# The opening of a two-block network on one core: token norm between the modulation blocks, scaling on two engines, small loads behind a wait

## The chip, the cores and the metric

The kernel runs on one core of one Trainium2 chip. The metric is the device time of one execution in microseconds. The kernel before took 2512.3 us (median of 3 runs, 2510.04 to 2513.72).

## The reference

A first block (diffusion-transformer style) and two layers of a second block work on 256 tokens of width 1024. Only the opening of the first block matters here. A modulation vector is made from the condition, `silu(c) @ w_ada + b_ada`, for the latent tokens and for the context tokens; its first 1024 values are a shift and the next 1024 a scale. Then

```
h     = rmsnorm(x,   g_mix_pre) * (1 + scale)   + shift       # 256 latent tokens
h_ctx = rmsnorm(ctx, g_mix_pre) * (1 + scale_c) + shift_c     # 256 context tokens
p     = concat(h, h_ctx) @ w_in                               # keys, values, gates, queries
```

The neighbourhood attention that follows adds a small learned table of relative biases, `rpb` (8 heads, 15 x 31 values), to its scores. Behind it come a matrix memory branch, a mixture of 32 experts, and the second block.

## The kernel before

Every engine has its own program, written out by hand; the only ordering between engines is by semaphores. Whatever stands behind a wait on an engine waits too. Activations lie transposed, width on the partitions (8 chunks of 128) and tokens along the free axis: `hAll[:, c, 0:256]` is chunk c of the latent tokens, `hAll[:, c, 256:512]` of the context tokens.

Weights go through a ring of 6 places of 2 MB, all issued by SyncE in a fixed order (L578 to L584): ada0 to ada3 (the four blocks of w_ada that give shift and scale), na_k, na_v, then rel0, rel1 (a constant table), ml_k, ml_v, each of the last four when its place is free. Place n is free when the slab n - 6 has been used: rel0 waits for the modulation block 0, rel1 for 1, ml_k for 2, ml_v for 3. Ahead of them SyncE loads x and ctx (L576, L577). ScalarE issues some 35 small loads of vectors and constants (L642 to L654) and can compute only after them. GpSimd issues 16 loads of parts of `rpb` into the tile `relrhs` (L2293: 31 partitions by 6 elements of 4 bytes, 8 heads twice) and one of the gate biases `bg` (L2295), from the start of the kernel on. [...]

TensorE's order in the opening (L1030 to L1099) is this. It turns the vectors and the 8 chunks of tokens. Then come four modulation blocks: `ada(i)` is 16 matmul instructions of 512 columns on slab ada_i (L1046), ScalarE copies the sums (L664, `ada_copy`), `ada_turn(i)` is 8 narrow ones that turn the copy (L1054), and VectorE adds the bias (L1737, L1738, `modulation`). Behind all four stands the norm: 16 matmul instructions add the squares over the width (L1068), ScalarE copies (L676), 8 narrow ones turn the sums (L1072), VectorE adds epsilon (L1748), ScalarE takes the root (L678), VectorE the reciprocal (L1750), and 8 matmul instructions spread the result over the partitions (L1077). VectorE multiplies the tokens by it (L1753, L1754: 16 operations, `xn_done` per chunk), ScalarE applies scale and shift (L683 latent, L685 context: 16 operations, `h_done` per chunk). TensorE waits for all 8 chunks and then makes the projections: na_k in 4 tiles (L1084), na_v in 4 tiles (L1114), ml_k, ml_v, and so on. After tile na_v0 stands the first of seven groups of small matmuls that build the bias from `relrhs` and rel0 (L1099, `rel_group`); `rel_group(0)` waits for all 16 loads of `rpb`.

Of the kernel before, what the change touches and what calls it, by code (L numbers as in the profile page):

```python
# [10 lines left out]
ALU = mybir.AluOpType  # L11
ACT = mybir.ActivationFunctionType
# [3 lines left out]
D = 1024  # L16
DC = D // P
T = 256
# [6 lines left out]
EPS = 1e-6  # L25
# [112 lines left out]
def build(nc, A, out):  # L138

    with ExitStack() as ctx:  # L140
# [3 lines left out]
        def sem(name):  # L144
            return ctx.enter_context(nc.semaphore(name))


        bank = [ctx.enter_context(nc.psum_tensor(f"bank{i}", [P, 512], F32)) for i in range(8)]
# [10 lines left out]
        xT = sb("xT", [P, DC, T])  # L159
        vT = sb("vT", [P, NV1])  # L160
        v2T = sb("v2T", [P, 2 * NV2])
        mod = sb("mod", [P, 48])
        modc = sb("modc", [P, 16])
        gains = sb("gains", [P, 2, DC])
        stage = sb("stage", [P, 64])
        colA = sb("colA", [P, 8])
# [221 lines left out]
        n_sum = sem("n_sum")  # L388
        n_par = sem("n_par")
        n_parc = sem("n_parc")  # L390
        par_done = sem("par_done")
        par_copied = sem("par_copied")
        ada_rows = sem("ada_rows")
        ada_copied = sem("ada_copied")
# [56 lines left out]
        gains_done = sem("gains_done")  # L451
        sq_done = sem("sq_done")
        sum_done = sem("sum_done")
        ms_done = sem("ms_done")
        root_done = sem("root_done")
        rstd_done = sem("rstd_done")
        rstd_row = sem("rstd_row")
        xn_done = sem("xn_done")
        h_done = sem("h_done")
        lin_done = sem("lin_done")  # L460
# [170 lines left out]
        def _(act):  # L631
# [27 lines left out]
            def ada_copy(i):  # L659

                act.wait_ge(ada_rows, i + 1)
                if i:
                    act.wait_ge(lin_done, G1[f"ada{i - 1}"] + 1)
                act.activation(adaRow[i], bank[G1[f"ada{i}"] % 4][:, :], ACT.Copy).then_inc(ada_copied, 1)  # L664
# [5 lines left out]
                act.activation(sq[:, c, T:512], hAll[:, c, T:512], ACT.Square).then_inc(sq_done, 1)  # L670
            act.wait_ge(vecs_turned, 2)
            act.activation(v2T[:, :], bank[6][:, 0:2 * NV2], ACT.Copy).then_inc(v2_copied, 1)
            for i in range(4):
                ada_copy(i)
            act.wait_ge(par_done, 1)
            act.activation(rstd, bank[6][:, :], ACT.Copy).then_inc(par_copied, 1)  # L676
            act.wait_ge(ms_done, 1)
            act.activation(colA[:, 0:4], colA[:, 0:4], ACT.Sqrt).then_inc(root_done, 1)  # L678

            act.wait_ge(gains_done, 1)  # L680
            for c in range(DC):
                act.wait_ge(xn_done, c + 1)
                act.activation(hAll[:, c, 0:T], hAll[:, c, 0:T], ACT.Identity, bias=mod[:, c:c + 1],  # L683
                               scale=gains[:, 0, c:c + 1])
                act.activation(hAll[:, c, T:512], hAll[:, c, T:512], ACT.Identity, bias=modc[:, c:c + 1],  # L685
                               scale=gains[:, 1, c:c + 1]).then_inc(h_done, 1)

# [120 lines left out]
            for c in range(DC):  # L808
                act.wait_ge(n_xn, c + 1)
                act.activation(h2T[:, c, :], tmpx[:, c, :], ACT.Identity, bias=mod[:, 24 + c:25 + c],  # L810
                               scale=gpre[:, c:c + 1]).then_inc(h2_done, 1)
# [201 lines left out]
        def _(pe):  # L1013
# [18 lines left out]
            for c in range(DC):  # L1032
                if c >= 4:
                    pe.wait_ge(x_copied, 2 * (c - 4) + 2)
                for t in range(4):
                    last = pe.transpose(bank[c % 4][:, t * P:(t + 1) * P], xin[:, t, c * P:(c + 1) * P], K["ident"][:, :])
# [4 lines left out]
            def ada(i):  # L1041
                w = slab(f"ada{i}")
                b = open_bank(f"ada{i}")
                for c in range(DC):
                    r = 32 * (c % 4)
                    last = pe.matmul(b[r:r + 32, :], scol[:, c, :], w[:, c, :], start=(c < 4), stop=(c >= 4), skip_group_check=True)  # L1046
                last.then_inc(ada_rows, 1)

            def ada_turn(i):

                pe.wait_ge(ada_copied, i + 1)
                b = bank[G1[f"ada{i}"] % 4]
                for m in range(4):
                    last = pe.matmul(b[:, 2 * m:2 * m + 2], adaRow[i][:, m * P:(m + 1) * P], K["pick"][:, :], start=True, stop=True)  # L1054
                last.then_inc(lin_done, 1)

            pe.wait_ge(silu_done, 1)
            for i in range(4):
                ada(i)
                if i:  # L1060
                    ada_turn(i - 1)
            ada_turn(3)

            pe.wait_ge(sq_done, DC)
            pe.wait_ge(v2_copied, 1)
            for c in range(DC):
                r = 32 * (c % 4)
                last = pe.matmul(bank[6][r:r + 32, :], ones[:, 0:32], sq[:, c, :], start=(c < 4), stop=(c >= 4), skip_group_check=True)  # L1068
            last.then_inc(par_done, 1)
            pe.wait_ge(par_copied, 1)  # L1070
            for t in range(4):
                last = pe.matmul(bank[6][:, t:t + 1], rstd[:, t * P:(t + 1) * P], K["pick"][:, 0:1], start=True, stop=True)  # L1072
            last.then_inc(sum_done, 1)

            pe.wait_ge(rstd_done, 1)
            for t in range(4):
                last = pe.matmul(bank[5][:, t * P:(t + 1) * P], colA[:, t:t + 1].to_broadcast([P, P]), K["ident"][:, :],  # L1077
                                 start=True, stop=True)
            last.then_inc(rstd_row, 1)

            def feat(name, w, m, half, rhs, dst, kc=DC, base=0):

                for c in range(kc):
                    last = pe.matmul(dst, w[:, c, base + m * P:base + (m + 1) * P], rhs(c), start=(c == 0), stop=(c == kc - 1))  # L1084
                return last

            for c in range(DC):
                pe.wait_ge(h_done, c + 1)
            def rel_group(b):

                if b == 0:
# [244 lines left out]
            for g in range(4):  # L1336
                pe.wait_ge(lin_act, emptied(G1["out3"])[1])
                for k in range(4):
                    c = 4 * (g % 2) + k
# [366 lines left out]
        def _(dve):  # L1706
# [23 lines left out]
            def modulation(i):  # L1730

                g = G1[f"ada{i}"]
                ps = bank[g % 4][:, 0:8].rearrange("p (m a) -> p m a", a=2)
                vb = vT[:, ba + 4 * i:ba + 4 * i + 4]
                dve.wait_ge(lin_done, g + 1)
                if i < 4:
                    dve.tensor_tensor(modc[:, 4 * i:4 * i + 4], ps[:, :, 1], vb, ALU.add)  # L1737
                dve.tensor_tensor(mod[:, 4 * i:4 * i + 4], ps[:, :, 0], vb, ALU.add).then_inc(lin_dve, 1)  # L1738

            for i in range(4):  # L1740
                modulation(i)
            dve.wait_ge(*emptied(G1["ada3"]))
            dve.scalar_tensor_tensor(out=gains[:, 0, :], in0=mod[:, 8:16], scalar=1.0, in1=vcol("g_mix_pre"),
                                     op0=ALU.add, op1=ALU.mult)
            dve.scalar_tensor_tensor(out=gains[:, 1, :], in0=modc[:, 8:16], scalar=1.0, in1=vcol("g_mix_pre"),
                                     op0=ALU.add, op1=ALU.mult).then_inc(gains_done, 1)
            dve.wait_ge(sum_done, 1)
            dve.tensor_scalar(colA[:, 0:4], bank[6][:, 0:4], 1.0 / D, EPS, ALU.mult, ALU.add).then_inc(ms_done, 1)  # L1748
            dve.wait_ge(root_done, 1)
            dve.reciprocal(colA[:, 0:4], colA[:, 0:4]).then_inc(rstd_done, 1)  # L1750
            dve.wait_ge(rstd_row, 1)
            for c in range(DC):
                dve.tensor_tensor(hAll[:, c, 0:T], xT[:, c, :], bank[5][:, 0:T], ALU.mult)  # L1753
                dve.tensor_tensor(hAll[:, c, T:512], hAll[:, c, T:512], bank[5][:, T:512], ALU.mult).then_inc(xn_done, 1)  # L1754

            dve.memset(mlV[:, :, 128:129], 1.0).then_inc(ones_set, 1)

# [527 lines left out]
        @block.gpsimd  # L2285
        def _(pool):

            pool.wait_ge(ones_set, 1)
            src = A["rpb"][0].rearrange("h r d -> d h r")
            with nc.allow_non_contiguous_dma(reason="a small table turned"):  # L2290
                for a in range(2):
                    for h in range(NA_H):
                        pool.dma_start(relrhs[31 * a:31 * a + 31, 6 * h:6 * h + 6], src[:, h, 5 - a:11 - a])\  # L2293
                            .then_inc(relrhs_in, 16)
                pool.dma_start(bg[:, :], A["b_mlstm_gates"][0].rearrange("a b -> (a b)").partition_broadcast(P)).then_inc(bg_in, 16)  # L2295

            pool.wait_ge(na_os, NA_H)
            for w, n in enumerate(("b_gate", "b_lin", "b_down")):
                for k in range(2):
                    src = A[n][0][:, 512 * k:512 * k + 512][None, :, :].to_broadcast([2, E, 512])  # L2300
                    pool.dma_start(braw[64 * k:64 * k + 64, w, :], src).then_inc(moe_const, 16)
            pool.wait_ge(ml_o, 2 * ML_H)
            pool.wait_ge(lin_done, G1["b_na3"] + 1)
            pool.dma_start(posi.bitcast(I32), A["positions_2"][0].partition_broadcast(P)).then_inc(pos_in, 16)
            pool.dma_start(wr, A["w_router"][0].rearrange("(c p) n -> p c n", p=P)).then_inc(moe_const, 16)
            pool.dma_start(brow, A["b_router"][0].partition_broadcast(P)).then_inc(moe_const, 16)
            for L in range(2):
                pool.dma_start(gaRaw[:, L, :].rearrange("p (c n) -> p c n", c=DC),
                               A["w_in_2"][L][:, C2["ga"]:C2["ga"] + GR].rearrange("(c p) n -> p c n", p=P)).then_inc(moe_const, 16)
            pool.wait_ge(ml_hts, ML_H)  # L2310
            pool.dma_start(biaspick, A["biaspick"]).then_inc(moe_const, 16)

            pool.wait_ge(bias_hi, 1)
            for k in range(2):
                r = slice(64 * k + 32, 64 * k + 64)
                pool.tensor_tensor(bparts[r, :, :], braw[r, :, :], bparts[r, :, :].bitcast(F32), ALU.subtract).then_inc(bias_lo, 1)
# [17 lines left out]
```

## Time and profile before

| | us |
|---|---|
| median of 3 runs | 2512.3 |
| profiled execution, whole | 2512.79 |
| its span in the profile | 2511.0 |
| TensorE busy | 2284.8 (91%) |
| VectorE busy | 752.2 (30%) |
| ScalarE busy | 636.0 (25%) |
| GpSimd busy | 44.8 (2%) |
| first projection (na_k) starts at | 67.83 |
| first bias group (`rel_group(0)`) starts at | 104.53 |

The span begins with the first instruction of the profile; the whole execution is 1.8 us longer. A matmul of 32-bit operands appears as two instructions (x16 for 8 chunks). [...] The opening is the first 105 us, 4% of the span.

### The profile page before, as it was taken

Reading aid. Unit: us, or ns where it says so; the run is one execution under the profiler, and the core shown is the slowest. Engines: PE = TensorE matmul, PEld = TensorE weight load, DVE = VectorE, ACT = ScalarE, POOL = GpSimd, SP = SyncE. Lnnn points to the kernel's source line nnn. Section 1 sums busy time; section 2 is a strip of 40 time slices with the busy share of each in tenths; the row PEclk is TensorE's granted clock in tenths of the full one; section 3 lists DMA queues with packets and bytes.
Section 4 is the critical chain, followed back from the end, with each engine's and each line's share of the span. In section 5 each row is a group of like instructions: output and inputs, shape, how many; then the busy total and the mean of one; then the engine's idle time right before and its main releaser. Section 6 shows DMA issues by size and latency. Waiting matters only on the chain.

```text
span 2511.0 us, 31285 instructions
## 1 busy us (share of the span) xinstructions
PE 2284.8 (91%) x13158; PEld 1564.7 (62%) x13158; DVE 752.2 (30%) x1189; ACT 636.0 (25%) x900; POOL 44.8 (2%) x35
## 2 busy tenths in 40 slices
PE   4999998789889988988898889999999799998998
PEld 2458667533333333333333379998899699987997
DVE  1001225321111111111111156433444454442453
ACT  2101432211111111111111144422333435413432
POOL 2100000100000000000000000000000000000000
PEclk8898999799999999999999989999899899998999
DMA  9434354279999999999999966671245345541542
GB/s 285 86 118 168 137 211 126 83 308 427 428 428 427 428 428 427 427 427 429 424 428 427 400 138 167 149 255 67 101 168 185 107 163 164 193 148 68 184 160 93
DMA packets 133833, 626.99 MB, mean 250 GB/s; under 512 B 9344, under 2 KB 17040, under 8 KB 108864
## 3 DMA queue, kind: packets, MB, share of 16 engines
q1 hardware_dynamic: 128672, 622.51, 65.4%
q0 software_dynamic: 2912, 1.44, 1.0%
q8 instruction: 112, 1.84, 0.3%
q10 hardware_dynamic: 2112, 0.99, 0.2%
q14 instruction: 25, 0.20, 0.0%
HBM read 623.69 MB, written 1.05 MB: 249 GB/s over the span
## 4 chain that ended last, share of the span: by engine, by line
PE 72%; DMA 20%; DVE 3%; issue 3%; ACT 2%; ACTq 0%; SPq 0%; DVEq 0%
DMA ring<-in_w_lin 17%; PE bank L1365 15%; PE bank L1084 13%; PE bank L1463 11%; PE bank L1663 10%; PE bank L1678 4%; PE bank L1114 2%; DMA ring<-in_w_ada 1%; PE bank L1487 1%; DMA ring<-in_w_in 1%; PE bank L1472 1%; PE bank L1378 1%; PE bank L1353 1%; PE bank L1179 1%; PE bank L1046 1%
## 5 line engine op out<-in xcount | busy, mean ns | idle before, releaser
L1365 PE MATMUL bank<-ring,arenaA 128*64 128x512 f32 x3072 | 692.4, 601 | 38.9 <-DMA ring<-in_w_lin 29.4
L1365 PEld LDWEIGHTS bank<-ring,arenaA 128*64 128x64 f32 x3072 | 211.5, 138 | 460.7 <-issue 392.2
L1084 PE MATMUL bank<-arenaA,ring 128*128 128x256 f32 (+1 forms) x1408 | 345.1, 405 | 14.5 <-ACT arenaA L685 9.2
L2091 DVE TENSOR_TENSOR ring_rounded<-ring,ring_rounded 128x2048 fp32r<-128x2048 f32 (+1 forms) x140 | 293.4, 2134 | 114.7 <-ACT ring_rounded L864 114.7
L1084 PEld LDWEIGHTS bank<-arenaA,ring 128*128 128x128 f32 x1408 | 270.7, 195 | 88.9 <-issue 38.6
L864 ACT ACTIVATE ring_rounded<-ring 128x2048 fp32r<-128x2048 f32 (+1 forms) x140 | 243.2, 1783 | 299.5 <-DMA ring<-in_w_in 81.8
L1463 PE MATMUL bank<-arena_rounded,ring_rounded 128*128 128x256 f32 x2496 | 308.1, 283 | 1.7 <-DVE ring_rounded L2091 1.7
L1463 PEld LDWEIGHTS bank<-arena_rounded,ring_rounded 128*128 128x128 f32 x2496 | 300.1, 190 | 6.0 <-issue 3.1
L1663 PE MATMUL bank<-arena_rounded,ring_rounded 128*128 128x256 f32 x2112 | 260.4, 287 | 2.2 <-ACT arena_rounded L989 2.2
L1663 PEld LDWEIGHTS bank<-arena_rounded,ring_rounded 128*128 128x128 f32 x2112 | 258.5, 194 | 4.3 <-ACT arena_rounded L989 2.8
L2037 DVE TENSOR_SCALAR arenaA<-bank 128x512 f32<-128x512 f32 x32 | 22.1, 692 | 504.1 <-PE bank L1365 504.1
L1678 PE MATMUL bank<-arena_rounded,ring_rounded 128*128 128x256 f32 x912 | 109.9, 283 | 2.3 <-DVE arenaA L2270 2.3
L1678 PEld LDWEIGHTS bank<-arena_rounded,ring_rounded 128*128 128x128 f32 x912 | 109.5, 192 | 2.7 <-issue 2.7
L879 ACT ACTIVATE arenaA<-bank 128x512 f32<-128x512 f32 (+1 forms) x88 | 51.3, 586 | 226.6 <-PE bank L1463 120.8
L845 ACT ACTIVATE arenaA<-bank 128x512 f32<-128x512 f32 x32 | 19.1, 597 | 330.7 <-PE bank L1409 330.7
L849 ACT ACTIVATE arenaA<-bank 64x512 f32<-64x512 f32 x64 | 37.9, 592 | 213.6 <-PE bank L1365 213.2
L843 ACT ACTIVATE arenaA<-arenaA 128x512 f32<-128x512 f32 x32 | 20.2, 630 | 264.3 <-DVE arenaA L2037 264.3
L2049 DVE TENSOR_SCALAR arenaA<-bank 128x512 f32<-128x512 f32 x32 | 22.1, 692 | 203.7 <-PE bank L1365 203.7
L1378 PE MATMUL bank<-arenaA 128*128 128x256 f32 x256 | 63.5, 392 | 7.8 <-ACT arenaA L849 5.5
L1378 PEld LDWEIGHTS bank<-arenaA 128*128 128x128 f32 x256 | 45.7, 189 | 32.4 <-issue 18.7
L1297 PE MATMUL bank<-arenaA,ones 128*32 128x256 f32 x176 | 32.5, 501 | 31.9 <-ACT arenaA L775 24.9
L1359 PE MATMUL bank<-arena_rounded 128*128 128x512 f32 x96 | 45.2, 471 | 17.8 <-issue 17.1
(338 smaller groups left out, 1658.8 us busy)
## 6 DMA issues: line engine op xcount, KB each, us to landing
ring<-in_w_gate SPq DMA_DIRECT2D x64, 2048.0 KB, 22.9
ring<-in_w_lin SPq DMA_DIRECT2D x64, 2048.0 KB, 25.3
ring<-in_w_down SPq DMA_DIRECT2D x64, 2048.0 KB, 21.7
ring<-in_w_in SPq DMA_DIRECT2D x41, 2048.0 KB, 10.7
ring<-in_w_ada SPq DMA_DIRECT2D x12, 2048.0 KB, 15.5
ring<-in_w_ffn_gate SPq DMA_DIRECT2D x10, 2048.0 KB, 7.8
ring<-in_w_ffn_up SPq DMA_DIRECT2D x10, 2048.0 KB, 7.7
ring<-in_w_ffn_down SPq DMA_DIRECT2D x12, 1536.0 KB, 6.6
```

The costliest lines, as they stand in the source:

```text
L849: ins = act.activation(yN[(i % 2) * SLOTS:(i % 2 + 1) * SLOTS, k, :], bank[5][k * SLOTS:(k + 1) * SLOTS, :], ACT.Copy)
L864: act.activation(place2(name + "_hi", ringR)[:, a:b, :], place2(name)[:, a:b, :], ACT.Copy).then_inc(w_hi, 1)
L879: act.activation(dst, src(b) if src else b, func, scale=scale).then_inc(c_act, 1)
L1084: last = pe.matmul(dst, w[:, c, base + m * P:base + (m + 1) * P], rhs(c), start=(c == 0), stop=(c == kc - 1))
L1114: last = pe.matmul(b[:, :], hAll[:, c, m * P:(m + 1) * P], w[:, c, :], start=(c == 0), stop=(c == DC - 1))
L1359: pe.matmul(bank[b][:, :], bias, bparts[:, w, :], start=True, stop=False, skip_group_check=True)
L1365: last = pe.matmul(bank[b][k * SLOTS:(k + 1) * SLOTS, :], lhsT(c), slot(j)[:, c % 4, k * 512:(k + 1) * 512], start=False, stop=(c == DC - ...
L1378: last = pe.matmul(bank[6 + g % 2][:, k * T:(k + 1) * T], yN[:, c // 4, (c % 4) * P:(c % 4 + 1) * P], selWT, start=True, stop=True)
L1463: last = pe.matmul(b[:, j * T:(j + 1) * T], w[:, c, m * P:(m + 1) * P], h[:, c, :], start=(part == 0 and c == 0 and j == 0), stop=(part == ...
L1663: last = pe.matmul(b[:, j * T:(j + 1) * T], w[:, c, m * P:(m + 1) * P], h[:, c, :], start=(part == 0 and c == 0 and j == 0), stop=(part == ...
L1678: last = pe.matmul(bank[m // 2][:, (m % 2) * T:(m % 2 + 1) * T], w[:, k, m * P:(m + 1) * P], h[:, c0 + k, :], start=(part == 0 and c0 + k ...
L2091: dve.tensor_tensor(place2(name, ringR)[:, a:b, :], w[:, a:b, :], hi[:, a:b, :], ALU.subtract).then_inc(w_lo, 1)
```

## The change

TensorE's order becomes: ada(0); sums of squares; ada(1), turn 0; turn of the sums; ada(2), turn 1; spread of the reciprocal; ada(3), turn 2, turn 3. ScalarE, VectorE follow this order. The scaling of the latent half goes from ScalarE to VectorE (new semaphore `h_lat`); ScalarE keeps the context half. The first tile of na_k waits for each chunk just before its matmul, no longer for all eight. GpSimd waits for `ada_rows` to reach 4, which the last matmul of ada(3) brings about, before it issues its 16 + 1 small loads.

```diff
 # ScalarE
-            for i in range(4):
-                ada_copy(i)
-            act.wait_ge(par_done, 1)
+            ada_copy(0)
+            act.wait_ge(sum_done, 1)
             act.activation(rstd, bank[6][:, :], ACT.Copy).then_inc(par_copied, 1)
+            ada_copy(1)
             act.wait_ge(ms_done, 1)
             act.activation(colA[:, 0:4], colA[:, 0:4], ACT.Sqrt).then_inc(root_done, 1)
+            ada_copy(2)
+            ada_copy(3)
             act.wait_ge(gains_done, 1)
             for c in range(DC):
                 act.wait_ge(xn_done, c + 1)
-                act.activation(hAll[:, c, 0:T], hAll[:, c, 0:T], ACT.Identity, bias=mod[:, c:c + 1],
-                               scale=gains[:, 0, c:c + 1])
                 act.activation(hAll[:, c, T:512], ...).then_inc(h_done, 1)
 # TensorE
-            for i in range(4):
-                ada(i)
-                if i:
-                    ada_turn(i - 1)
-            ada_turn(3)
-
+            ada(0)
             pe.wait_ge(sq_done, DC)
             pe.wait_ge(v2_copied, 1)
...
-            last.then_inc(par_done, 1)
+            last.then_inc(sum_done, 1)
+            ada(1)
+            ada_turn(0)
             pe.wait_ge(par_copied, 1)
...
             last.then_inc(sum_done, 1)
+            ada(2)
+            ada_turn(1)
             pe.wait_ge(rstd_done, 1)
...
-            last.then_inc(rstd_row, 1)
+            last.then_inc(sum_done, 1)
+            ada(3)
+            ada_turn(2)
+            ada_turn(3)
             def feat(name, w, m, half, rhs, dst, kc=DC, base=0):
                 for c in range(kc):
+                    if name == "na_k" and m == 0:
+                        pe.wait_ge(h_done, c + 1)
+                        pe.wait_ge(h_lat, c + 1)
                     last = pe.matmul(...)
-            for c in range(DC):
-                pe.wait_ge(h_done, c + 1)
 # VectorE
-            for i in range(4):
-                modulation(i)
+            modulation(0)
+            dve.wait_ge(sum_done, 2)
+            dve.tensor_scalar(colA[:, 0:4], bank[6][:, 0:4], 1.0 / D, EPS, ALU.mult, ALU.add).then_inc(ms_done, 1)
+            modulation(1)
+            dve.wait_ge(root_done, 1)
+            dve.reciprocal(colA[:, 0:4], colA[:, 0:4]).then_inc(rstd_done, 1)
+            dve.wait_ge(sum_done, 3)
+            for c in range(DC):
+                dve.tensor_tensor(hAll[:, c, 0:T], xT[:, c, :], bank[5][:, 0:T], ALU.mult)
+                dve.tensor_tensor(hAll[:, c, T:512], hAll[:, c, T:512], bank[5][:, T:512], ALU.mult).then_inc(xn_done, 1)
+            modulation(2)
+            modulation(3)
             (gains as before)
+            dve.wait_ge(gains_done, 1)
+            dve.wait_ge(xn_done, DC)
             for c in range(DC):
+                dve.tensor_scalar(hAll[:, c, 0:T], hAll[:, c, 0:T], gains[:, 0, c:c + 1], mod[:, c:c + 1], ALU.mult, ALU.add)\
+                    .then_inc(h_lat, 1)
 # GpSimd
             pool.wait_ge(ones_set, 1)
+            pool.wait_ge(ada_rows, 4)
             (the 16 loads of rpb, the load of bg)
```

## Rows read from the trace of the kernel before

**Rows 1.** Page, chain that ended last: shares of the span by engine, by line.
```profile
PE 72%; DMA 20%; DVE 3%; issue 3%; ACT 2%; ACTq 0%; SPq 0%; DVEq 0%
DMA ring<-in_w_lin 17%; PE bank L1365 15%; PE bank L1084 13%; PE bank L1463 11%; PE bank L1663 10%; PE bank L1678 4%; PE bank L1114 2%; DMA ring<-in_w_ada 1%; PE bank L1487 1%; DMA ring<-in_w_in 1%; PE bank L1472 1%; PE bank L1378 1%; PE bank L1353 1%; PE bank L1179 1%; PE bank L1046 1%
```
**Rows 2.** Chain in order of time, 0 to 260 us: start, length, what.
```profile
15.14 30.33 DMA ring<-in_w_ada
...
51.61 3.42 PE bank L1068 x16
...
67.83 29.90 PE bank L1084 x64
97.73 6.87 PE bank L1114 x16
104.60 2.36 PE bank L1099 x20
```
**Rows 3.** Timeline of TensorE: start, length, line, tiles, [idle before <- releaser].
```profile
26.10 1.92 PE L1046 MATMUL bank<-ring,scol 128*32 128x512 f32 x16 [1.18 <-DVE arenaA L1726]
30.06 2.48 PE L1046 MATMUL bank<-ring,scol 128*32 128x512 f32 x16 [2.03 <-DMA ring<-in_w_ada]
32.46 1.87 PE L1054 MATMUL bank<-k_pick,arenaA 128*128 128x2 f32 x8
35.97 3.64 PE L1046 MATMUL bank<-ring,scol 128*32 128x512 f32 x16 [1.64 <-DMA ring<-in_w_ada]
...
48.76 1.05 PE L1054 MATMUL bank<-k_pick,arenaA 128*128 128x2 f32 x8
...
57.46 1.16 PE L1077 MATMUL bank<-k_ident,colA 128*128 128x128 f32 x8 [0.71 <-DVE colA L1750]
```
**Rows 4.** Timeline of ScalarE, copy of v2T and first and last of 16 scalings.
```profile
26.62 0.24 ACT L672 ACTIVATE v2T<-bank 128x108 f32<-128x108 f32 x1
...
59.50 0.60 ACT L683 ACTIVATE arenaA<-arenaA,mod,gains 128x256 f32<-128x256 f32 x1 [2.31 <-DVE arenaA L1754]
...
66.89 0.58 ACT L685 ACTIVATE arenaA<-arenaA,modc,gains 128x256 f32<-128x256 f32 x1
```
**Rows 5.** Timeline of VectorE, first and last of 16 multiplications by the norm.
```profile
58.66 0.42 DVE L1753 TENSOR_TENSOR arenaA<-xT,bank 128x256 f32<-128x256 f32 x1 [1.25 <-PE bank L1077]
...
63.63 0.41 DVE L1754 TENSOR_TENSOR arenaA<-arenaA,bank 128x256 f32<-128x256 f32 x1
```
**Rows 6.** Timeline of GpSimd, five of the eight pairs of rpb loads.
```profile
1.41 3.73 POOL L2293 DMA_DIRECT2D arenaA<-in_rpb  x2 [0.95 <-DVE arenaA L1716]
15.60 3.53 POOL L2293 DMA_DIRECT2D arenaA<-in_rpb  x2 [10.46 <-issue]
...
71.66 3.53 POOL L2293 DMA_DIRECT2D arenaA<-in_rpb  x2 [11.18 <-issue]
84.99 3.53 POOL L2293 DMA_DIRECT2D arenaA<-in_rpb  x2 [9.80 <-issue]
93.67 3.52 POOL L2293 DMA_DIRECT2D arenaA<-in_rpb  x2 [5.14 <-issue]
```
**Rows 7.** DMA issues, us to landing: last rpb load (95.42), slab ml_v.
```profile
arenaA<-in_rpb POOLq DMA_DIRECT2D x1, 0.7 KB, 6.6
...
ring<-in_w_in SPq DMA_DIRECT2D x1, 2048.0 KB, 32.3
```
**Rows 8.** Windows: length, busy (count) by engine, PEclk, DMA share, GB/s.
```profile
8.00:11.00 3.00, 0.00 (x0) 0.00 (x0) 0.00 (x0) 0.00 (x0) 0.00 (x0) 1.00 0.99 118
...
15.00:21.00 6.00, 1.41 (x7) 1.01 (x5) 0.59 (x4) 3.04 (x4) 3.53 (x2) 1.00 1.07 369
21.00:25.00 4.00, 3.55 (x17) 3.33 (x17) 4.00 (x13) 3.65 (x12) 0.00 (x0) 1.00 1.24 117
...
35.00:39.00 4.00, 3.03 (x16) 0.59 (x16) 0.00 (x0) 0.03 (x1) 0.00 (x0) 0.50 1.30 114
```
**Rows 9.** The same windows view, TensorE's clock.
```profile
31.50:48.50 17.00, 11.25 (x56) 4.75 (x48) 0.46 (x4) 1.20 (x2) 5.08 (x3) 0.50 1.11 308
...
67.80:72.50 4.70, 4.67 (x6) 2.06 (x7) 0.00 (x0) 0.00 (x0) 0.84 (x1) 0.53 0.92 301
```

More of the change, by code:

```diff
@@ L390, in build @@
         n_parc = sem("n_parc")
-        par_done = sem("par_done")
         par_copied = sem("par_copied")
@@ L456, in build @@
         rstd_done = sem("rstd_done")
-        rstd_row = sem("rstd_row")
+        h_lat = sem("h_lat")
         xn_done = sem("xn_done")
@@ L1746, in _ @@
                                      op0=ALU.add, op1=ALU.mult).then_inc(gains_done, 1)
[L1747 to L1751, printed above, removed]
+            dve.wait_ge(gains_done, 1)
+            dve.wait_ge(xn_done, DC)
             for c in range(DC):
-                dve.tensor_tensor(hAll[:, c, 0:T], xT[:, c, :], bank[5][:, 0:T], ALU.mult)
-                dve.tensor_tensor(hAll[:, c, T:512], hAll[:, c, T:512], bank[5][:, T:512], ALU.mult).then_inc(xn_done, 1)
+                dve.tensor_scalar(hAll[:, c, 0:T], hAll[:, c, 0:T], gains[:, 0, c:c + 1], mod[:, c:c + 1], ALU.mult, ALU.add)\
+                    .then_inc(h_lat, 1)
             dve.memset(mlV[:, :, 128:129], 1.0).then_inc(ones_set, 1)
```

## The prediction

> **What bounds the kernel now.** I read the page first. The chain that ended last is 72% TensorE, 17% the stream of expert weights [rows 1]. There the reader sees that nothing on the page is about the opening: the change can only shift the moment from which everything behind it runs. So the question is when TensorE gets past the opening, and next I read the chain in order of time. It has two parts. Up to 45.5 us it waits for the fourth slab of w_ada (15.14 + 30.33 = 45.47), then runs the norm, one short step after another, and the scaling, until the first projection starts at 67.83. From there to 104.60 TensorE does nothing but projections, and then the first bias group [rows 2]. No DMA stands on this chain between 67.83 and 258 us, and the expert weights cannot start before their places are used by TensorE; so a shift of the moment at which the first bias group starts (104.6) passes on to the end in full.
>
> The third view is the timeline of GpSimd, an engine that the page shows at 2%. It issues the rpb loads in pairs, and between pairs it waits 5 to 11 us, put down to "issue" [rows 6]. The last load is issued at 95.42 (93.67 + half of 3.52) and lands 6.6 us later [rows 7], at 102.0. The bias group waits for all 16 and starts at 104.6: the loads, though they start at 1.41, have only 2.6 us to spare. This is the fact on which the forecast rests.
>
> The fourth view is the windows with the GB/s. Weights flow at 369 GB/s in 15 to 21 us, and at 118, 117 and 114 in 8 to 11, 21 to 25 and 35 to 39 us [rows 8], each about 6 us after a pair of rpb loads was begun. The small loads slow the slabs.
>
> **The change part by part.** Times are of the profiled execution (span 2511.0, whole 2512.8 us, 0.5 above the median of 2512.3).
>
> *Slabs come sooner.* Without rpb loads ahead of ada(3) the three slow stretches go: 3 x (1 - 118/369) = 2.0, 4 x (1 - 117/369) = 2.7, 4 x (1 - 114/369) = 2.8 us [rows 8], 7.5 us together. The fourth slab then lands at 38.0, not 45.5. If the slow stretches had another cause it stays 45.5; I take 38.0, since each of the three follows a pair. The second and third slabs were waited for at 30.06 and 35.97 [rows 3]; with 4.7 us less each (two stretches) they are there at 25.4 and 31.3.
>
> *TensorE's new order.* ada(0) can't start sooner than 26.10: it was released by VectorE's copies, not by a slab [rows 3]. It ends at 28.0. The squares are done (v2T copied at 26.9 [rows 4]), so the 16 matmuls of the sums follow, 1.9 us by ada(0)'s row, same shape, upper clock (3.42 at the lower [rows 2]): 29.9. ada(1) 1.9 (31.8), turn 0 1.05 (32.9), turn of the sums 1.05 by the same narrow form (33.9), ada(2) 1.9 (35.8), turn 1 1.05 (36.9), some 0.4 for modulation(1) and the reciprocal on VectorE, spread 1.2 [rows 3] (38.6), ada(3) 1.9: 40.5. With the lower clock, which was there from 31.5 to 48.5 [rows 9], the forms take 3.5 and 1.87 us (35.97 and 32.46 in [rows 3]): turn 0 33.7, turn of the sums 35.6, ada(2) 39.1, turn 1 41.0, spread about 43.2, ada(3) 46.7. Before the clock fell TensorE had waited for a slab; here it has hardly a gap from 26.1 on, so I take the upper: `ada_rows` is 4 at 41, bounds 39 and 47. All waits of ScalarE (copy of the sums, root with its table load) and VectorE lie beside these matmuls; they would show as gaps of under 1 us each.
>
> *Behind ada(3).* Turn 2 to 41.6, the copy of block 3 (0.6 and 0.2 of gaps), turn 3 to 43.5. VectorE's 16 multiplications go at 0.33 us ((63.63 - 58.66)/15 [rows 5]), 38.7 to 44.1, then two modulations and the gains, 0.4. They hide behind the turns but for 0.6 us or so. Scaling: ScalarE had 16 operations at 0.49 ((66.89 - 59.50)/15 [rows 4]), 7.9 us up to 67.47 before TensorE moved. Now it has 8, VectorE's 8 are beside them. No row shows that VectorE operation; bounded by 0.3 us (its multiplication) and 0.6 (ScalarE's), one chunk takes less than the 0.86 us that TensorE needs for its two matmuls of a chunk (6.87/8 [rows 2]), so the chunkwise wait costs TensorE one chunk at the most, 0.6 us. na_k starts at 45.3 (52 with the lower clock), where it was 67.83. Taken alone that is a gain of 15 to 22 us. From there five tiles at 6.87 us: TensorE stands at the bias group at 79.7 to 89.
>
> *The rpb loads, behind `ada_rows` >= 4.* They start at 41, not at 1.41. While slabs flow, a pair comes every 13.9 us ((84.99 - 1.41)/6); the one interval after the slabs were over is 8.7 us (84.99 to 93.67) [rows 6]. The slabs ended at 84.0 (ml_v is issued when the turn of block 3 is over, 51.6 [rows 2], and takes 32.3 to landing [rows 7]). They will end about 73, since in place of six pairs some two fall among them (four times 2.7). So the pairs start at 41, 54.9, 68.8, then with one mixed interval of 10 at 79, and at 87.7, 96.4, 105.1, 113.8; the last load is issued at 115.6 and lands at 122.2. TensorE stands still from about 80 to 122, and everything it gained is idle time. Nothing else can go ahead of the bias group on TensorE: na_v1 to the end are queued behind it, and ScalarE and VectorE wait for their banks. The group starts 17.6 us later than at 104.6.
>
> *The clock.* After the 9 us pause before 67.83 TensorE ran at 0.53 until 72.5 [rows 9]; the first four tiles took 29.90 us instead of 4 x 6.87 = 27.5, 2.4 lost [rows 2]. In the chain of before this loss stood ahead of 104.6; now a pause of 40 us stands right at the group, and I add 2.4 behind it (bounds 0 and 5).
>
> *Sum.* +17.6 + 2.4 = +20 us: 2512.8 + 20 = 2532.8, by the median 2532.
>
> [...]
>
> **Rivals.**
> (a) *The loads keep up, and the change is faster.* With nothing before them in the queues they may go faster than any pair of the trace did. From the start at 41, seven intervals and 8.4 us to the last landing (1.8 + 6.6): the result is no change in time when the landing is at 102.2 (104.6 less the 2.4 of the clock), which needs (102.2 - 41 - 8.4)/7 = 7.5 us a pair. [...] For it: only one interval without slabs is in the trace. Against it: that one is 8.7, and its parts leave little room (3.5 to issue the pair, the wait of 5.14 until the second has landed).
> (b) *No difference that can be told.* A pair of 6.5 to 8.2 us, 2512.3 within 5.
> (c) *The front is as slow as before and the loads still later.* The clock stays at the lower level from 31.5 on, `ada_rows` is 4 at 47, three intervals are of the loaded kind: 47 + 3 x 13.9 + 4 x 8.7 + 8.4 = 131.9, +27.3 and up to 5 of clock: 2545.
> (d) *All intervals are short.* 39 + 7 x 8.7 + 8.4 = 108.3, +3.7 + 2.4: 2518.
>
> **Chances.** The forecast with its neighbours (c) and (d), slower by 6 to 32 us, 0.86; (a) 0.10; (b) 0.04. A difference under 0.2% (5 us) can't be told from none. The likeliest is 2532, and the range 2517 to 2545 goes from (d) to (c) and leaves out (a) and (b), 14 in 100, and little more. Faster 0.10, same 0.04, slower 0.86.
>
> **What would show it.** In the profile after: ada(1) and ada(2) without waits for slabs, the fourth slab in by 38, GB/s near 370 without the low stretches until about 47; na_k starting at 45 to 52; GpSimd's first pair at about 41 and its last at about 114; TensorE with one idle stretch of 30 to 45 us before L1099, and at the lower clock for some us behind it; from there to the end the same length as before. I am wrong if that idle stretch is short or absent, which would be seen at once in pairs less than 7.5 us apart, or if part of the stall is given back later, which no row speaks for.

## The result and the profile after

The changed kernel took 2525.0 us (median of 5 runs, 2523.0 to 2530.0); the kernel before, measured with it on the same chip, 2510.5. The ratio is 1.0054, with a 95% interval of 1.0043 to 1.0066: 11 to 17 us slower. The forecast was 2532, slower. The profiled execution took 2523.0 us, its span is 2521.2 (2511.0 before). Two executions far off all others of their kernels, one of `e2_wait_only` (4531 us) and one of `e4_rows_old_order` (10334 us), are left out below.

First the timeline of TensorE after the change, opening only: start, length, line, tiles, count, and in brackets the idle time ahead and its releaser.

```profile
24.27 1.92 PE L1045 MATMUL bank<-ring,scol 128*32 128x512 f32 x16 [0.87 <-DVE arenaA L1727]
...
27.70 1.93 PE L1045 MATMUL bank<-ring,scol 128*32 128x512 f32 x16
...
31.44 1.92 PE L1045 MATMUL bank<-ring,scol 128*32 128x512 f32 x16
...
35.84 1.92 PE L1045 MATMUL bank<-ring,scol 128*32 128x512 f32 x16
...
42.78 30.30 PE L1087 MATMUL bank<-arenaA,ring 128*128 128x512 f32 x64 [2.23 <-DVE arenaA L1761]
72.91 7.03 PE L1115 MATMUL bank<-ring,arenaA 128*128 128x512 f32 x16
119.30 4.50 PE L1100 MATMUL bank<-arenaA,ring 63*128 63x48 f32 x20 [39.36 <-DMA arenaA<-in_rpb]
123.73 8.50 PE L1115 MATMUL bank<-ring,arenaA 128*128 128x512 f32 x16
```

The four modulation blocks (L1045) no longer wait for slabs; compare [rows 3]. The first projection starts at 42.78, 25 us sooner than in [rows 2], and TensorE is ready for the bias group at 79.9. Then it stands still for 39.36 us, until the last load of `rpb` (the small table of relative biases) has landed, and starts the group at 119.30: 14.8 us later than before, 104.5.

The timeline of GpSimd, to be held against [rows 6]:

```profile
38.59 3.73 POOL L2302 DMA_DIRECT2D arenaA<-in_rpb  x2 [38.13 <-PE bank L1045]
54.64 3.53 POOL L2302 DMA_DIRECT2D arenaA<-in_rpb  x2 [12.33 <-issue]
67.73 3.53 POOL L2302 DMA_DIRECT2D arenaA<-in_rpb  x2 [9.57 <-issue]
76.42 3.52 POOL L2302 DMA_DIRECT2D arenaA<-in_rpb  x2 [5.16 <-issue]
...
111.00 3.52 POOL L2302 DMA_DIRECT2D arenaA<-in_rpb  x2 [5.04 <-issue]
```

The pairs begin at 38.59 instead of 1.41; two intervals are long (16.1 and 13.1 us), the other five are 8.6 to 8.7. This chain is on the path to the end now, as the chain of waits of the changed kernel shows (start, length, what):

```profile
38.59 3.73 POOL arenaA L2302 x2
42.31 12.33 issue
...
111.00 1.75 POOL arenaA L2302
112.75 6.50 DMA arenaA<-in_rpb
119.30 4.50 PE bank L1100 x20
```

The windows (columns as in [rows 8]) show the weight stream at 387 GB/s up to the wait's end, the low stretch of 68 that begins 6 us after the pair of 54.64, and the pause:

```profile
29.00:41.00 12.00, 10.39 (x88) 6.57 (x80) 5.76 (x22) 3.28 (x5) 2.41 (x2) 1.00 1.05 387
...
60.50:63.50 3.00, 3.00 (x9) 1.33 (x8) 0.00 (x0) 0.00 (x0) 0.00 (x0) 1.00 1.24 68
...
82.00:119.00 37.00, 0.00 (x0) 0.00 (x0) 0.00 (x0) 0.00 (x0) 14.68 (x9) 0.50 0.48 3
119.00:124.00 5.00, 4.70 (x21) 4.61 (x22) 0.16 (x1) 0.00 (x0) 0.00 (x0) 0.50 0.00 0
```

PEclk, TensorE's granted clock, is 1.00 at what the prediction calls the upper clock and 0.50 at the lower: the same 16 matmuls of a modulation block took 1.92 us at 1.00 (31.44 above) and 3.64 at 0.50 (35.97 in [rows 3]).

Does the delay reach the end? SyncE's issues of the expert slabs (MOVE lines: first one is expert 1's) and of the second block's gate slabs are good milestones, since each is released by TensorE. Before:

```profile
L590 SPq MOVE ring<-in_w_gate x62: 29/29/29, 518.2 to 1392.9; - x62
L619 SPq DMA_DIRECT2D ring<-in_w_ffn_gate x12: 367/368/582, 1679.1 to 2392.5; - x12
```

After:

```profile
L589 SPq MOVE ring<-in_w_gate x62: 29/29/29, 533.3 to 1408.2; - x62
L618 SPq DMA_DIRECT2D ring<-in_w_ffn_gate x12: 367/368/582, 1694.6 to 2402.9; - x12
```

The delay is 14.8 us at the first bias group, 18.2 at the second (132.16 against 113.95), 16.5 from the third on (141.58 against 125.07), 15.1 at expert 1, 15.3 at the last, 15.5 at the second block. So it is passed on nearly whole. Within the second block this one execution wins 5.1 us back (708.3 us from first to last gate slab, 713.4 before), so that its span is only 10.2 longer; the medians differ by 14.5. The code there is the same, and in the runs this part varies from kernel to kernel, 701 to 714 us.

### The profile page after: what moved, and what is told of

It reads as the page before. It is cut to its first block, busy times and chain, and to the rows that moved or that the text cites. A ratio compares the mean times of both kernels' runs of the same rounds, so it can differ in the third digit from the quotient of the medians.

```text
span 2521.2 us, 31291 instructions
## 1 busy us (share of the span) xinstructions
PE 2278.9 (90%) x13158; PEld 1563.7 (62%) x13158; DVE 754.7 (30%) x1197; ACT 631.6 (25%) x892; POOL 44.7 (2%) x35
## 4 chain that ended last, share of the span: by engine, by line
PE 68%; DMA 20%; issue 4%; DVE 3%; ACT 2%; POOL 1%; ACTq 1%; DVEq 0%; POOLq 0%
DMA ring<-in_w_lin 19%; PE bank L1366 14%; PE bank L1087 12%; PE bank L1464 11%; PE bank L1664 10%; PE bank L1679 4%; PE bank L1115 2%; PE bank L1488 1%; POOL arenaA L2302 1%; DMA ring<-in_w_in 1%; PE bank L1045 1%; PE bank L1473 1%; PE bank L1379 1%; PE bank L1180 1%; PE bank L1691 1%
## 5 line engine op out<-in xcount | busy, mean ns | idle before, releaser
L2045 DVE TENSOR_SCALAR arenaA<-bank 128x512 f32<-128x512 f32 x32 | 22.1, 692 | 502.0 <-PE bank L1366 502.0
L844 ACT ACTIVATE arenaA<-bank 128x512 f32<-128x512 f32 x32 | 19.1, 597 | 331.4 <-PE bank L1410 331.4
L848 ACT ACTIVATE arenaA<-bank 64x512 f32<-64x512 f32 x64 | 37.8, 591 | 213.7 <-PE bank L1366 213.3
L2057 DVE TENSOR_SCALAR arenaA<-bank 128x512 f32<-128x512 f32 x32 | 22.1, 692 | 204.4 <-PE bank L1366 204.4
L1379 PE MATMUL bank<-arenaA 128*128 128x256 f32 x256 | 63.5, 392 | 7.8 <-ACT arenaA L848 5.5
L691 ACT ACTIVATE arenaA<-bank 128x512 f32<-128x512 f32 x27 | 16.1, 597 | 197.1 <-PE bank L1115 106.2
```

Source lines behind the costliest of these rows:

```text
L848: ins = act.activation(yN[(i % 2) * SLOTS:(i % 2 + 1) * SLOTS, k, :], bank[5][k * SLOTS:(k + 1) * SLOTS, :], ACT.Copy)
L1379: last = pe.matmul(bank[6 + g % 2][:, k * T:(k + 1) * T], yN[:, c // 4, (c % 4) * P:(c % 4 + 1) * P], selWT, start=True, stop=True)
```

## The experiments

Ratios are to the kernel before, measured beside it on the same chip. Semaphore calls that the edits of the loads carry along are left out of the code shown. "Group" is the start of the first bias group (104.5 before, 119.3 after).

**e1_no_wait: the change without its wait.**

```diff
-            pool.wait_ge(ada_rows, 4)
```

> The changed kernel with GpSimd's wait for ada_rows >= 4 taken out: the 16 rpb loads start at 1.4 us again, all other edits stay. Theory A (the rpb loads are a chain of eight pairs that alone sets when the first bias group can start, and it was 2.6 us from doing so before the change): the last load lands at about 102, TensorE stands idle for 10 to 20 us in front of the first bias group, which starts at 102 to 104 us where it was 104.5; with 1 to 2 us lost to the lower clock behind the idle stretch the time is that of the kernel before, 2508 to 2512, 0.999 to 1.001 of it. Rival B (the reordering brings its 15 to 22 us and the wait alone spoils it): the group starts at 80 to 90 us and the time is about 2490 to 2496, 0.992 to 0.994.

Measured: 2506.8 us, 0.9983 (0.9972 to 0.9993). Timeline of TensorE:

```profile
54.26 29.92 PE L1087 MATMUL bank<-arenaA,ring 128*128 128x512 f32 x64 [2.63 <-DVE arenaA L1761]
84.01 7.03 PE L1115 MATMUL bank<-ring,arenaA 128*128 128x512 f32 x16
100.21 4.50 PE L1100 MATMUL bank<-arenaA,ring 63*128 63x48 f32 x20 [9.18 <-DMA arenaA<-in_rpb]
```

The group starts at 100.2, when the last load has landed, not at 91. So rival B falls: of the 13.6 us by which na_k is sooner, 4.3 come through. In the kernel before the group did not wait for the loads, but they were so close behind that any larger gain in front of it ran into them. They landed about 2 us sooner than expected, the pairs being a little closer (the last starts at 91.87 instead of 93.67), and the time lies just under the range of theory A.

**e2_wait_only: the kernel before with the wait.**

```diff
+            pool.wait_ge(ada_rows, 4)
```

> The kernel before with one line of the change, GpSimd's wait for ada_rows >= 4. Theory A: the fourth slab lands at 37 to 38, ada(3) ends at 40 to 42, the pairs start there and need 72 us to the first pair's last plus 8.4 to land; first bias group at 119 to 123, time that of the changed kernel or up to 3 us more, 2524 to 2529, though the norm still stands behind the modulation. Rival C (the harm of the change comes from its new order, for instance the clock or VectorE's added work): this kernel gains 7 us from the sooner slabs and is at 2503.

Measured: 2529.6 us, 1.0072 (1.0059 to 1.0085). Timeline of TensorE:

```profile
117.29 4.50 PE L1099 MATMUL bank<-arenaA,ring 63*128 63x48 f32 x20 [23.32 <-DMA arenaA<-in_rpb]
```

The wait alone makes the whole loss; rival C falls. The group is 2 us sooner than theory A had it, since GpSimd's first pair starts at 36.52. That it is at least as slow as the full change, with its group 2 us sooner than there, is not explained; the two intervals overlap.

**e3_rows and e3_again: the change without the wait, with cheap loads.** The table is loaded as 48 rows of 31 contiguous values, twice, and turned on TensorE in front of na_k.

```diff
-                    for h in range(NA_H):
-                        pool.dma_start(relrhs[31 * a:31 * a + 31, 6 * h:6 * h + 6], src[:, h, 5 - a:11 - a])
+                    pool.dma_start(relrow[0:48, 31 * a:31 * a + 31], A["rpb"][0][:, 5 - a:11 - a, :])
+            pe.transpose(bank[4][0:62, 0:48], relrow[0:48, 0:62], K["ident"][0:48, 0:48])
+            dve.tensor_copy(relrhs[0:62, :], bank[4][0:62, 0:48])
```

> The changed kernel without GpSimd's wait, and with rpb loaded by rows: two loads of 48 rows of 31 contiguous values (96 pieces of 124 bytes) in place of 16 loads of 186 pieces of 4 bytes, turned by one TensorE instruction and copied by VectorE (0.5 us in all). Theory A: no low stretches in the weight stream, no stall before the first bias group, which starts at 79 to 82 us; 23 to 26 us sooner than in the kernel before, and passed on in full: 2485 to 2489, 0.990 to 0.991. Rival D (what is won in the opening is given back before the experts, by a slab, a constant or the clock): the group starts at 80 and the end comes less than 15 us sooner, over 2496.

> The same kernel as e3_rows (the changed kernel without GpSimd's wait, rpb by rows), for a second measurement beside e9_rows_with_wait: 0.988 of the kernel before, 2480 to 2486. If it is over 2490, the 11 us between it and e6_rows_scaling_undone came from the runs and not from the scaling.

Measured: 2484.8 us, 0.9881 (0.9865 to 0.9897), and again 2484.3 us, 0.9889 (0.9868 to 0.9910). This beats both kernels. Timeline of e3_rows:

```profile
44.99 29.66 PE L1090 MATMUL bank<-arenaA,ring 128*128 128x512 f32 x64 [1.54 <-DVE arenaA L1764]
74.48 7.03 PE L1118 MATMUL bank<-ring,arenaA 128*128 128x512 f32 x16
81.44 2.43 PE L1103 MATMUL bank<-arenaA,ring 63*128 63x48 f32 x20
```

No pause; the group starts 23.1 us sooner than before, and expert 1 comes 26.7 sooner (491.5 against 518.2; why that is more than 23.1 was not looked into). Nothing is given back: rival D falls.

**e9_rows_with_wait: the full change, wait included, with cheap loads.** The edit of e3_rows on the changed kernel, `pool.wait_ge(ada_rows, 4)` kept.

> The changed kernel whole, its wait for ada_rows included, but with rpb loaded by rows (two loads of 48 rows of 31 values, one TensorE turn in front of na_k). If the wait does harm only through the long chain behind it: the two loads land some 7 us after the wait opens (38.6), at 45 to 47, TensorE's turn waits for them, na_k starts 1 to 4 us later than in e3_rows (45.0), time 2485 to 2490. Rival J (starting these loads late costs by itself, by slabs in flight or by waits elsewhere): over 2495.

Measured: 2483.3 us, 0.9889 (0.9872 to 0.9906). Timeline of TensorE:

```profile
44.37 0.28 PE L1082 MATMUL bank<-k_ident,arenaA 48*62 48x48 f32 x1 [3.83 <-DMA arenaA<-in_rpb]
44.58 30.29 PE L1090 MATMUL bank<-arenaA,ring 128*128 128x512 f32 x64
```

GpSimd issues at 38.55, TensorE waits 3.83 us for the turn and starts na_k at 44.58, no later than in e3_rows (44.99). The wait itself is harmless; what hurts is the chain of eight pairs behind it. Rival J falls.

**e4_rows_old_order: cheap loads in the kernel before.** The same three edits, old order of the opening.

> The kernel before, in its old order, with rpb loaded by rows as in the run above. It tells what the sooner slabs bring by themselves. Theory A: the fourth slab lands at 37 instead of 45.5, norm and scaling follow as before, na_k starts at about 59 and the first bias group at 95 to 96: 8 to 10 us faster, 2501 to 2503, 0.996 to 0.997; so of the gain of the run above some 9 us are the slabs and 15 the new order. Rival E (the low stretches of the weight stream have another cause than the rpb loads): the fourth slab still lands at 45 and the time is 2510.

Measured: 2503.3 us, 0.9962 (0.9949 to 0.9975). Timeline:

```profile
35.80 2.83 PE L1047 MATMUL bank<-ring,scol 128*32 128x512 f32 x16 [2.51 <-DMA ring<-in_w_ada]
...
59.46 29.95 PE L1087 MATMUL bank<-arenaA,ring 128*128 128x512 f32 x64 [9.05 <-ACT arenaA L686]
...
96.21 2.43 PE L1102 MATMUL bank<-arenaA,ring 63*128 63x48 f32 x20
```

The fourth slab is there at 35.80 instead of 45.52 with no 4-byte pieces beside it, and the weights flow at 365 GB/s in 21 to 25 us and at 387 in 35 to 39, where the kernel before fell to 117 and 114 [rows 8]. This settles that the low stretches were the rpb loads' doing (rival E falls), and splits the 23 us of e3_rows: 8.3 (104.53 - 96.21) from the loads alone, 14.8 from the new order and the chunkwise wait.

**e6_rows_scaling_undone and e11_rows_chunkwise_act: which part of the rest works.** Both stand on e3_rows. In e6 ScalarE scales both halves and TensorE waits for all chunks; in e11 ScalarE scales both, but TensorE waits chunk by chunk.

```diff
+                act.activation(hAll[:, c, 0:T], hAll[:, c, 0:T], ACT.Identity, bias=mod[:, c:c + 1], scale=gains[:, 0, c:c + 1])
-                dve.tensor_scalar(hAll[:, c, 0:T], ..., ALU.mult, ALU.add).then_inc(h_lat, 1)
 # e6 only
-                    if name == "na_k" and m == 0:
-                        pe.wait_ge(h_done, c + 1)
+                    if name == "na_k" and m == 0 and c == 0:
+                        pe.wait_ge(h_done, DC)
```

> The kernel e3_rows with two parts of the change undone: ScalarE scales both halves (16 operations), TensorE waits for all 8 chunks before na_k. Theory A: with the loads out of the way these parts are on the path: na_k started at 45.0 in e3_rows, now 16 operations at 0.49 us and 0.4 of latency later, 51.5 to 53; 7 to 8 us slower than e3_rows, 2491 to 2494, 0.991 to 0.992 of the kernel before. Rival G (the scaling hides, or the clock takes the difference): within 3 us of e3_rows, 2485 to 2488.

> The kernel e3_rows with one part of the change undone: ScalarE scales both halves again, but TensorE still waits chunk by chunk in the first tile of na_k. Theory A: TensorE begins 1.0 us after the gains (two operations), and ScalarE's 0.98 us per chunk is 0.12 more than TensorE's 0.86, so the whole costs 1 to 2 us against e3_rows, and the chunkwise wait alone is worth nearly all of the 7 us that e6_rows_scaling_undone lost: 2485 to 2488, 0.989 to 0.991. Rival M (the split of the scaling is what brings the gain): 2489 to 2493, 0.991 to 0.993.

Measured: e6 0.9936 (0.9920 to 0.9951), e11 0.9898 (0.9883 to 0.9913), e3_rows 0.9881 and 0.9889. Timeline of e6:

```profile
39.84 1.05 PE L1056 MATMUL bank<-k_pick,arenaA 128*128 128x2 f32 x8 [0.75 <-ACT arenaA L664]
40.82 0.23 PE L1084 MATMUL bank<-k_ident,arenaA 48*62 48x48 f32 x1
50.35 29.28 PE L1091 MATMUL bank<-arenaA,ring 128*128 128x512 f32 x64 [9.30 <-ACT arenaA L687]
```

and of e11:

```profile
39.97 1.05 PE L1056 MATMUL bank<-k_pick,arenaA 128*128 128x2 f32 x8 [0.75 <-ACT arenaA L664]
40.95 0.23 PE L1084 MATMUL bank<-k_ident,arenaA 48*62 48x48 f32 x1
43.63 29.20 PE L1091 MATMUL bank<-arenaA,ring 128*128 128x512 f32 x64 [2.45 <-ACT arenaA L687]
```

With turn 3 at the same moment (39.84, 39.97), na_k starts 6.7 us later without the chunkwise wait. With it, the split of the scaling over two engines makes no difference that can be told: in e3_rows 3.3 us lie between turn 3's start and na_k's (41.70 to 44.99), in e11 3.7. Theory A holds against G and M in what it says of na_k, and for the time of e11. The time of e6 is 11 us over e3_rows, more than the 7 to 8 of theory A. Its profiled execution is 4.8 behind at expert 1 (496.3 against 491.5; e3_rows had PEclk 0.50 in 19 to 28 us, where e6 had 1.00) and 4.5 at the end (span 2488.9 against 2484.4); the rest of the medians' difference is open.

**e5b_larger_store and e8_quarter_store: what sets the pace of the pairs.** The changed kernel with another `dynamic_dma_scratch_size`. The expectation of e8 calls it GpSimd's descriptor store, and here it is "the store"; what the runs show of it is how many loads GpSimd issues before it pauses. In e5b four small tiles and four constant tables were moved into an unused part of the arena to make room. (e8 has half the store; "quarter" in its label is wrong.) There is no time for `e5_half_store`: with 16384 bytes, and not the half that its label and expectation name, it left the arena 95840 bytes a partition where it needs 103232.

```diff
-    nc = _bacc.Bacc("TRN2", ..., dynamic_dma_scratch_size=8192)
+    nc = _bacc.Bacc("TRN2", ..., dynamic_dma_scratch_size=12288)   # e8: 4096
```

> The changed kernel with dynamic_dma_scratch_size=12288; to make room, a few small first-block tiles and constants lie in an unused part of the arena. [...] Rival F: pairs or not, the last load lands at 119 again and the time is 2525.

> The changed kernel with GpSimd's descriptor store halved, dynamic_dma_scratch_size=4096 in place of 8192 (one load of 186 pieces fits). Theory A2 (the store sets how many loads are in flight): single loads, some 6 us apart with the slabs over and 10 beside them; 38.6 + 3 x 10.3 + 12 x 6.1 + 5.7 = 148 us to the last landing, first bias group 25 to 32 us later than in the changed kernel (119.3), time 2550 to 2557, 1.015 to 1.018 of the kernel before. Rival F (the store is no bound): as the changed kernel, 2525.

Timeline of GpSimd in e5b, then in e8:

```profile
40.59 7.24 POOL L2306 DMA_DIRECT2D arenaA<-in_rpb  x4 [40.14 <-PE bank L1049]
63.13 7.04 POOL L2306 DMA_DIRECT2D arenaA<-in_rpb  x4 [15.31 <-issue]
79.17 7.03 POOL L2306 DMA_DIRECT2D arenaA<-in_rpb  x4 [9.00 <-issue]
93.48 7.04 POOL L2306 DMA_DIRECT2D arenaA<-in_rpb  x4 [7.28 <-issue]
```

```profile
40.22 1.94 POOL L2302 DMA_DIRECT2D arenaA<-in_rpb  x1 [39.77 <-PE bank L1045]
51.95 1.80 POOL L2302 DMA_DIRECT2D arenaA<-in_rpb  x1 [9.80 <-issue]
...
132.75 1.77 POOL L2302 DMA_DIRECT2D arenaA<-in_rpb  x1 [3.99 <-issue]
138.54 1.77 POOL L2302 DMA_DIRECT2D arenaA<-in_rpb  x1 [4.02 <-issue]
```

Fours with 12288 bytes, pairs with 8192, singles with 4096: the store sets how many loads of 186 pieces (31 x 6 elements) are in flight. GpSimd goes on when they have landed: with the slabs over, a load of e8 lands 5.4 to 5.6 us after its issue, and the next one is issued after 5.7 to 5.9. Rival F falls. What a piece takes of the store can be estimated from these counts: three loads (558 pieces) did not fit in 8192 bytes, and four (744) fitted in 12288, so it is between 14.7 and 16.5 bytes. Per load that is 14.3/4 = 3.6, 8.7/2 = 4.3 and 5.8 us with the slabs over. Groups at 107.4, 119.3 and 144.1. e8 took 2553.1 us, 1.0156 (1.0136 to 1.0177), as forecast. e5b took 2502.9 us, 0.9971 (0.9961 to 0.9982): 22.1 us less than the changed kernel, of which its sooner group explains 11.9 (119.3 - 107.4).

**e10_tiles_moved: why e5b is too fast.** The kernel before with only the tiles moved.

> The kernel before, its order, its rpb loads and its store of 8192 as they were, with only the small tiles moved into the arena as in e5b_larger_store. That run came out 8 to 15 us faster than its bias group allows; most of it lay in the second block (701 us from its first to its last gate slab, 713 in the kernel before). Theory K (where the tiles lie does it): this kernel is 8 to 12 us faster than the kernel before, 0.995 to 0.997. Rival L (the second block varies with the time at which it begins, whatever the tiles): 0.999 to 1.001.

Measured: 2505.8 us, 0.9974 (0.9965 to 0.9983), group at 106.54. About 6 us are the tiles' place (or the changed order of the constant loads that went with it), between K and L, although this group too is 2.0 us later than before. e5b's group is only 0.9 us later than this one, and its ratio (0.9971) is the same within the intervals: by the times, the moved tiles account for what was too fast in e5b. The profiles do not agree on where. In e10 3.5 us are won between the group and expert 1 (516.7) and 5.2 in the second block, 708.2 us long (1676.0 to 2384.2); in e5b all is won in the second block, 701.1 us long. And the changed kernel, its tiles in their old place, took 708.3 us there. The cause stays open.

**e7_sync_queue: the same 4-byte loads on SyncE's queue.** Issued between ada3 and na_k.

```diff
+                if n == 4:
+                    for a in range(2):
+                        for h in range(NA_H):
+                            sp.dma_start(relrhs[31 * a:31 * a + 31, 6 * h:6 * h + 6], tab[:, h, 5 - a:11 - a])
```

> The changed kernel without GpSimd's wait, and the same 16 rpb loads of 4-byte pieces issued by SyncE between the slabs ada3 and na_k. Theory H (the software queue's store and landing waits are what makes the loads slow; on the hardware queue they are issued back to back, and cost the DMA engines at most 2.7 us each, 43 us beside the slabs): all landed before TensorE needs them at 80 to 85, SyncE's later slabs some 10 to 25 us late but still before their use; time 2485 to 2500. Rival I (4-byte pieces are slow on any queue, and now stand ahead of na_k in the same queue): na_k lands late, at 65 to 85 instead of 43 to 51, TensorE waits for it, and the time is 2505 to 2530.

Measured: 2500.2 us, 0.9959 (0.9944 to 0.9974). SyncE's timeline and the DMA engines' share while it issues:

```profile
19.30 33.41 SPq L586 DMA_DIRECT2D arenaA<-in_rpb  x16
52.75 1.71 SPq L591 DMA_DIRECT2D ring<-in_w_in  x2
```

```profile
36.00:54.00 18.00, 4.16 (x34) 2.37 (x33) 8.62 (x31) 4.64 (x9) 0.00 (x0) 0.64 0.08 1
```

The loads take 2.1 us each to issue, and once the earlier slabs are in, the DMA engines have next to nothing to do (share 0.08): SyncE is the bound, and na_k's slab stands behind it. TensorE waits 20.50 us for that slab, na_k starts at 61.51, the group at 97.80. Rival I had the place right (na_k late, just before its 65 to 85) but not the price. H's time was right at its edge, and the rpb loads landed in time as it said; that SyncE's later slabs would still come before their use was wrong.

## Why the prediction was right, point by point

**The bound.** That the rpb chain had only 2.6 us to spare, and that a later start would make it the bound, is shown from both sides: e2 (wait alone) has the whole loss, e9 (wait with cheap loads) none. The passing on of the delay is shown by the milestones, 15.1 us at expert 1 for 14.8 at the group. The prediction named as a sign of being wrong that part of the stall is given back later; of the 18.2 us at the second group, 3.1 are by expert 1, and in the profiled execution 5.1 more in the second block, where the medians' 14.5 speaks for the delay of 15 staying whole.

**Slabs.** The three low stretches were blamed on the rpb loads and priced at 7.5 us. e4 shows 9.7 for the fourth slab (45.52 to 35.80): the cause was right, the price a little low. Some 1.6 us of it are a wait that the sum left out: SyncE holds slabs two to four back until ScalarE's vectors are in, and these came sooner too, so that the fourth was issued at 13.49 us instead of 15.14; the rest of the difference was not traced.

**TensorE's order and the clock in it.** I had `ada_rows` at 4 at 41; it was there at 37.8, and GpSimd's first load started at 38.59. The step that failed is "ada(0) can't start sooner than 26.10": in this program VectorE's copies wait for ScalarE, and ScalarE computes only when it has issued its small loads. It was through with them at 15.39 instead of 17.23, and ada(0) began 1.8 us sooner, at 24.27. The upper clock held through the modulation blocks, as chosen (1.92 us each, where the lower had 3.64), and the gaps were under 1 us as forecast: 0.41 before the spread, 0.75 before turn 3, while the root's table load, 1.28 us long, lay beside ada(2). TensorE stood at the bias group at 79.9, where the forecast had 79.7, by two misses that cancel: na_k began 2.5 us sooner than forecast, and the five tiles took 37.2 us, not 34.4, as TensorE ran at the lower clock from 43 to 48 us (PEclk 0.50). The prediction had seen such a loss before and not carried it over.

**The pairs.** First to last pair 72.4 us (38.59 to 111.00), forecast 72.8. Last issue to group 6.55 us, forecast 6.6. Reading the one interval of 8.7 us as the pace with the slabs over was right. That the whole fits so well is partly luck: the first three intervals were 16.1, 13.1 and 8.7 where the forecast had 13.9, 13.9 and 10, and the sums are the same.

**The sum.** Group +14.8 where I had +17.6: 2.4 of the difference are the start at 38.6 instead of 41, 0.4 the pairs. The clock term was mis-sized. Behind the pause the group took 4.50 us instead of 2.43 and the next tile 8.50 instead of 7.13, 3.4 together where I had 2.4. But the kernel before has short stretches at the lower clock in the same part: its third tile took 8.83 us (PEclk 0.83 from 115 to 125 us), the same tile after the change had the upper clock (PEclk 1.00 from 133 to 141 us) and took 1.7 less. By expert 1 only 0.3 us of the loss is left (15.1 - 14.8). So 20 became 15; the median says 14.5.

**The gains that were hidden.** The 15 to 22 us of the forecast were for na_k's start, sooner slabs included. Taken free of the loads it is 22.8 us sooner (67.83 to 44.99, e3), the upper end. At the group, of 23.1 us the slabs bring 8.3 and the new order with the chunkwise wait 14.8 (e4, e3). Nearly half of the 14.8 is the chunkwise wait alone (6.7, e6 against e11).

**Rivals.** (a), that the loads would keep up, is refuted: five intervals of 8.6 to 8.7 us where it needed 7.5, 3.5 of issuing and 5.0 to 5.2 of waiting each. From issue to landing one such load took 5.4 to 6.6 us with the queues empty (e8 and the kernel before), 6.5 for the last one after the change. Even the row loads of e4 and e9 took 5.0 to 5.9 us. (b), (c) and (d) did not come: two intervals were long, and PEclk was 1.00 in 29 to 41 us. (b) was also drawn too wide: at its 6.5 us a pair the last load lands at 95, and by the prediction's own sum the kernel is some 7 us faster, not within 5.

## What to carry to other kernels

GpSimd, which the profile shows at 2%, held TensorE in front of the first bias group for 39.4 us here: before a load is put behind a wait, ask when its last piece lands now and what its slack is (2.6 us here), not how long one issue takes (1.8 us). The 4-byte pieces on GpSimd's queue cost three times in this kernel: their own chain, whose pace followed the store (5.8, 4.3 and 3.6 us a load with 4096, 8192 and 12288 bytes), the weight stream beside them (8.3 us at the group, e4), and TensorE, which waited. It is worth trying to fetch such a table in contiguous rows and turn it on TensorE; here that alone turned a change worth +14 us into one worth -28.

## What the runs showed of the hardware

- A store of 4096, 8192 or 12288 bytes let one, two or four loads of 186 pieces be in flight (e8, the changed kernel, e5b).
- Beside a pair of such loads the weight stream fell from 387 GB/s (29 to 41 us) to 68 for 3 us (changed kernel, 60.5 to 63.5 us). On SyncE's queue the same loads left the DMA engines at a share of 0.08 (e7, 36 to 54 us), but held SyncE for 2.1 us each.
- In these traces a matmul of plain 32-bit operands left two instructions (kernel before, L1046: x16 for 8 matmuls), but one of rounded 32-bit operands left one (L1359: x96 for 3 in each of 32 experts).
- The second block, the same code in all kernels, took 701 to 714 us from its first to its last gate slab. The kernel with a few small tiles moved is 6 us faster in the whole (e10); why was not found.
